# Expert blocks of a hybrid decoder: moving the weight halves between GpSimd, ScalarE and VectorE, and turning the inner rows inside the next gate product

## The reference, cut to what matters

```python
row_tok = jnp.zeros((rows,), jnp.int32).at[dest].set(flat_t[order])
xb = xf[row_tok].reshape(n_blocks, MOE_BLOCK, -1)          # 128 rows x 1024

def expert_block(args):
    xblk, e = args
    return (jax.nn.silu(xblk @ w_gate[e]) * (xblk @ w_up[e])) @ w_down[e]
```

## Time and profile before

| what | value |
|---|---|
| median of three runs | 3995.15 us (3989.59 to 3999.66) |
| time of the profiled execution | 3984.88 us |
| its span, from first to last instruction | 3983.0 us |
| PE busy over the span | 3255.6 us (82%) |
| DVE busy | 1890.7 us (47%) |
| ACT busy | 1362.0 us (34%) |
| POOL busy | 655.6 us (16%) |
| mean granted clock of PE | 0.903 |

### The profile page before, as it was taken

How to read it: one execution, slowest core, us unless ns; L and a number is a source line. 1 busy time by engine, 2 the same in 40 slices (tenths; PEclk the granted TensorE clock), 3 DMA queues, 4 the chain that set the end, 5 groups by cost and what they waited for, 6 DMA issues and landing times. The chain is left out here.

```text
span 3983.0 us, 61834 instructions
## 1 busy us (share of the span) xinstructions
PE 3255.6 (82%) x22582; PEld 2717.2 (68%) x22583; DVE 1890.7 (47%) x2705; ACT 1362.0 (34%) x2830; POOL 655.6 (16%) x425
## 2 busy tenths in 40 slices
PE   7999999899959995486799867885188998989980
PEld 7999999788858884343577725774167777777760
DVE  5252455455535554211466522332377666665634
ACT  5121354355536563032133223442033333333310
POOL 1000000000000001130000010110433534443323
PEclk9999999899979997697899977886599999999995
DMA  4334332334521112353233232222287776776749
GB/s 166 114 108 157 122 109 91 101 118 126 164 85 47 55 50 70 101 184 120 85 120 120 90 109 90 96 93 68 105 290 254 265 282 251 268 271 217 275 167 337
DMA packets 309938, 591.64 MB, mean 149 GB/s; under 512 B 80597, under 2 KB 136323, under 8 KB 309230
## 3 DMA queue, kind: packets, MB, share of 16 engines
q1 hardware_dynamic: 250846, 365.54, 27.7%
q0 software_dynamic: 47776, 196.29, 13.6%
q10 hardware_dynamic: 11136, 27.27, 1.7%
HBM read 462.13 MB, written 160.44 MB: 156 GB/s over the span
## 5 line engine op out<-in xcount | busy, mean ns | idle before, releaser
L136 PE MATMUL pj_pu<-pj_w,pj_nT 128*128 128x256 f32 (+3 forms) x1088 | 306.8, 282 | 0.0
L137 PE MATMUL pj_pu<-pj_w,pj_nT 128*128 128x256 f32 (+3 forms) x1088 | 305.9, 281 | 0.0
L138 PE MATMUL pj_pu<-pj_w,pj_nT 128*128 128x256 f32 (+3 forms) x1088 | 305.3, 281 | 0.0
L2999 POOL TENSOR_TENSOR ex_down<-ex_down_raw,ex_down 128x2048 fp32r<-128x2048 f32 x32 | 212.0, 6625 | 506.9 <-ACT ex_down L3082 506.9
L3103 ACT ACTIVATE ex_y<-ex_py 128x512 f32<-128x512 f32 x96 | 52.2, 597 | 507.6 <-PE ex_py L138 507.6
L137 PEld LDWEIGHTS pj_pu<-pj_w,pj_nT 128*128 128x128 f32 (+1 forms) x1088 | 202.1, 186 | 0.0
L138 PEld LDWEIGHTS pj_pu<-pj_w,pj_nT 128*128 128x128 f32 (+1 forms) x1088 | 202.0, 186 | 0.0
L136 PEld LDWEIGHTS pj_pu<-pj_w,pj_nT 128*128 128x128 f32 (+1 forms) x1088 | 201.7, 185 | 0.1
L136 PE MATMUL ex_py<-ex_down,ex_hT 128*128 128x512 f32 x384 | 156.0, 406 | 40.1 <-POOL ex_down L2999 33.3
L716 ACT ACTIVATE att_prob<-att_score,att_res 128x256 f32<-128x256 f32 (+1 forms) x384 | 127.6, 444 | 144.2 <-DVE att_res L752 144.2
L136 PE MATMUL pj_pu<-pj_nT,pj_w 128*128 128x384 f32 (+2 forms) x480 | 175.3, 365 | 0.0
(11 more groups left out here) (581 smaller groups left out, 8436.6 us busy)
## 6 DMA issues: line engine op xcount, KB each, us to landing
ex_gate_raw<-in_w_gate SPq DMA_DIRECT2D x32, 2048.0 KB
ex_up_raw<-in_w_up SPq DMA_DIRECT2D x32, 2048.0 KB, 11.2
ex_down_raw<-in_w_down POOLq DMA_DIRECT2D x32, 2048.0 KB, 9.3
tmp_yb<-ex_y ACTq DMA_DIRECT2D x48, 512.0 KB, 7.2
out_win_k<-in_cache_k POOLq DMA_DIRECT2D x8, 2032.0 KB, 12.9
out_win_v<-in_cache_v POOLq DMA_DIRECT2D x8, 2032.0 KB, 14.7
tmp_att<-att_res POOLq DMA_DIRECT2D x48, 264.0 KB, 4.6
pout_att<-tmp_att SPq DMA_DIRECT2D x16, 792.0 KB, 7.3
```

What stands on the lines that cost most here:

```text
L136: pe.matmul(out, ah, bh, start=start, stop=False)
L137: pe.matmul(out, ah, bl, start=False, stop=False)
L138: return pe.matmul(out, al, bh, start=False, stop=stop)
L2999: return eng.tensor_tensor(half["d"][:, 1, k], raw["d"][:, k], half["d"][:, 0, k].bitcast(F32), ALU.subtract)
```

## The change

GpSimd computes nothing any more in the loop: it issues gathers, index loads and the loads of d. ScalarE makes the upper half of g as well (`upper_gate`, for block b+2, once the gate product of block b+1 has been done), so it makes all upper halves. VectorE makes all lower halves, for d over all four k-slices. Every half is made in two instructions over half of the k-slices each (`part`), and PE waits for the two separately in the middle of the up and gate products. VectorE's order becomes `hh`, lower d, `hT`, lower u, `rows`, lower g of block b+2. On PE the turn of `hh` moves from ahead of the next gate product to its middle, behind 12 of its 24 matmuls, and PE waits for `sg_ok` before the gate product begins.

```diff
-        def lower_d(eng, n):
-
-            k = slice(n * KF // 2, (n + 1) * KF // 2)
-            return eng.tensor_tensor(half["d"][:, 1, k], raw["d"][:, k], half["d"][:, 0, k].bitcast(F32), ALU.subtract)
+        def part(p, h):
+
+            n = (KF if p == "d" else KD) // 2
+            return slice(h * n, h * n + n)
...
                         for piece, name in (("g", "w_gate"), ("u", "w_up")):
-                            sp.wait_ge(E[piece + "_split"], r)
+                            sp.wait_ge(E[piece + "_split"], 2 * r)
...
                 def work(i, u, b):
                     pool.wait_ge(E["x_turned"], b + 1)
                     gather(u, b + 2, i + 2)
-                    with pool.If(read(pool, 2, b, 1)):
-                        r = began(pool, b)
-                        pool.wait_ge(E["d_hi"], r)
-                        lower_d(pool, 0).then_inc(E["d_split"], 1)
                     with pool.If(read(pool, 2, b + 1, 1)):
                         e = read(pool, 0, b + 1, NE - 1)
-                        r = began(pool, b + 1)
-                        pool.wait_ge(E["d_split"], r)
-                        pool.sem_inc(E["seen"], 1)
-                        pool.wait_ge(E["d_split2"], r)
+                        pool.wait_ge(E["d_split"], 2 * began(pool, b + 1))
                         pool.sem_inc(E["seen"], 1)
                         load_down(e)
...
                 def upper(p, r):
                     act.wait_ge(E[p + "_in"], 16 * r)
-                    act.activation(half[p][:, 0], raw[p][:], ACT.Copy).then_inc(E[p + "_hi"], 1)
+                    for h in range(2):
+                        act.activation(half[p][:, 0, part(p, h)], raw[p][:, part(p, h)], ACT.Copy).then_inc(E[p + "_hi"], 1)
+
+                def upper_gate(b):
+                    with act.If(read(act, 2, b, 1)):
+                        r = began(act, b)
+                        act.wait_ge(E["gate_mm"], b)
+                        act.sem_inc(E["seen"], 1)
+                        upper("g", r)
+
+                upper("g", 1)
                 upper("u", 1)
+                upper_gate(1)
...
                         upper("u", r)
+                    upper_gate(b + 2)
                     act.wait_ge(E["y_mm"], b + 2)
...
-                def halves(p, r):
-                    dve.wait_ge(E[p + "_in"], 16 * r)
-                    split(dve, half[p][:, 0], half[p][:, 1], raw[p][:], E[p + "_hi"], r).then_inc(E[p + "_split"], 1)
-
                 def lower(p, r):
-                    dve.wait_ge(E[p + "_hi"], r)
-                    dve.tensor_tensor(half[p][:, 1], raw[p][:], half[p][:, 0].bitcast(F32), ALU.subtract).then_inc(E[p + "_split"], 1)
+                    for h in range(2):
+                        dve.wait_ge(E[p + "_hi"], 2 * r + h)
+                        dve.tensor_tensor(half[p][:, 1, part(p, h)], raw[p][:, part(p, h)], half[p][:, 0, part(p, h)].bitcast(F32),
+                                          ALU.subtract).then_inc(E[p + "_split"], 1)
+
+                def lower_if(p, b):
+                    with dve.If(read(dve, 2, b, 1)):
+                        lower(p, began(dve, b))
...
                 def work(i, u, b):
-                    with dve.If(read(dve, 2, b + 1, 1)):
-                        dve.wait_ge(E["gate_mm"], b + 1)
-                        halves("g", began(dve, b + 1))
                     dve.wait_ge(E["sg_ok"], b + 1)
                     dve.wait_ge(E["up_mm"], b + 1)
                     dve.wait_ge(E["h_turned"], b + 1)
                     dve.tensor_tensor(hh[:], sg[:], gu[:, 1, :], ALU.mult).then_inc(E["hh_ok"], 1)
-                    with dve.If(read(dve, 2, b, 1)):
-                        dve.wait_ge(E["d_hi"], began(dve, b))
-                        lower_d(dve, 1).then_inc(E["d_split2"], 1)
-                    rows(u, b + 2)
+                    lower_if("d", b)
                     dve.wait_ge(E["h_turned"], b + 2)
                     dve.wait_ge(E["y_mm"], b + 1)
                     split(dve, flat(hT[:, 0]), flat(hT[:, 1]), th[:], E["h_hi"], b + 1).then_inc(E["h_ok"], 1)
-                    with dve.If(read(dve, 2, b + 1, 1)):
-                        lower("u", began(dve, b + 1))
+                    lower_if("u", b + 1)
+                    rows(u, b + 2)
+                    lower_if("g", b + 2)
...
-                def project(p, u, n, b, sem):
-                    pe.wait_ge(E[p + "_split"], began(pe, b) + 1)
-                    for k in range(KD):
-                        last = matmul3(pe, gu[:, n, :], xT[:, u, 0, k, :], xT[:, u, 1, k, :], half[p][:, 0, k, :], half[p][:, 1, k, :],
-                                       k == 0, k == KD - 1)
+                def project(p, u, n, b, sem, between=None):
+                    r = began(pe, b)
+                    for h in range(2):
+                        pe.wait_ge(E[p + "_split"], 2 * r + 1 + h)
+                        if h and between:
+                            between()
+                        for k in range(KD)[part(p, h)]:
+                            last = matmul3(pe, gu[:, n, :], xT[:, u, 0, k, :], xT[:, u, 1, k, :], half[p][:, 0, k, :], half[p][:, 1, k, :],
+                                           k == 0, k == KD - 1)
                     last.then_inc(sem, 1)
...
+                    def turn_h():
+                        pe.wait_ge(E["hh_ok"], b + 2)
+                        for k in range(KF):
+                            last = pe.transpose(th[:, k * P:(k + 1) * P], hh[:, k * P:(k + 1) * P], ident[:])
+                        last.then_inc(E["h_turned"], 1)
+
                     project("u", u, 1, b, E["up_mm"])
                     turn(u, b + 2, i + 2)
-                    pe.wait_ge(E["hh_ok"], b + 2)
-                    for k in range(KF):
-                        last = pe.transpose(th[:, k * P:(k + 1) * P], hh[:, k * P:(k + 1) * P], ident[:])
-                    last.then_inc(E["h_turned"], 1)
-                    project("g", 1 - u, 0, b + 1, E["gate_mm"])
+                    pe.wait_ge(E["sg_ok"], b + 1)
+                    project("g", 1 - u, 0, b + 1, E["gate_mm"], turn_h)
                     r = began(pe, b)
                     pe.wait_ge(E["h_ok"], b + 1)
-                    pe.wait_ge(E["d_split"], r + 1)
-                    pe.wait_ge(E["d_split2"], r + 1)
+                    pe.wait_ge(E["d_split"], 2 * r + 2)
```

More of the change, by code:

```diff
@@ L2968, in experts @@
         py = s.ps("py", [P, 2, 512])
-        names = ("consts_in seen idx_in0 idx_in1 x_in0 x_in1 g_in u_in d_in g_hi u_hi d_hi g_split u_split d_split d_split2 x_turned x_hi x_ok "
+        names = ("consts_in seen idx_in0 idx_in1 x_in0 x_in1 g_in u_in d_in g_hi u_hi d_hi g_split u_split d_split x_turned x_hi x_ok "
                  "gate_mm up_mm sg_ok hh_ok h_turned h_hi h_ok y_mm y_ok y_out0 y_out1 zero_ok zero_out").split()
@@ L3113, in _ @@
             def _(dve):
-                for n in ("g_split", "u_split", "d_split", "d_split2", "hh_ok", "h_turned", "y_mm"):
+                for n in ("g_split", "u_split", "d_split"):
+                    dve.sem_inc(E[n], 2)
+                for n in ("g_hi", "u_hi", "d_hi", "hh_ok", "h_turned", "y_mm"):
                     dve.sem_inc(E[n], 1)
@@ L3131, in rows @@
                     split(dve, flat(xT[:, u, 0]), flat(xT[:, u, 1]), tr[:].rearrange("p k n -> p (k n)"), E["x_hi"], b + 1).then_inc(E["x_ok"], 1)
-                halves("g", 1)
+                lower("g", 1)
                 rows(0, 0)
@@ L3136, in _ @@
                 lower("u", 1)
+                lower_if("g", 1)
                 def work(i, u, b):
-                    with dve.If(read(dve, 2, b + 1, 1)):
-                        dve.wait_ge(E["gate_mm"], b + 1)
-                        halves("g", began(dve, b + 1))
                     dve.wait_ge(E["sg_ok"], b + 1)
```

## The result

The changed kernel took 3896.39 us (median of four, 3885.73 to 3906.32) against 3997.4 for the kernel before, measured beside it (3989.59 to 4006.11): a ratio of 0.9741, 95% interval 0.9713 to 0.9768. The forecast was 3916.

The account below looks back on a forecast made before the run. PE was taken to bound the expert stage. Gains of 9.3 (continuing blocks), 0.6 (last block), 20.5 (new blocks alone) and 48.8 (runs) made 79.2 us off, giving 3905.7 profiled and 3916 as median; range 3889 to 3962, forecast's own 3900 to 3932.

Parts of the forecast that it names:

- Continuing blocks: Fifteen blocks that continue an expert: PE's wait for hh goes, 17.70 us each, 265.5 in all, a gain of 9.3.
- New blocks alone: Nine new blocks standing alone: lower d on VectorE shortens the down product's wait; 18.71 us each, a gain of 20.5.
- rival 3: VectorE's plan reads hide after all, so every new block in a run takes 18.71 us: 3891 in all, chance 0.08.
- VectorE's ring in a run: With new blocks on end, VectorE's instructions and gaps take 20.05 us a block and replace PE as the bound.
- the forecast's 455.5: Time of all 23 new blocks in runs, against 504.3 us before, a gain of 48.8.
- The gathers: Gather issued at 15.6 us into a block, written by 20.5, landed at 24.2, on time for PE by 1.3.
- Rival 1, transfers: DMA transfers pace the runs: 3965 us if runs stay at 504.3, 3940 halfway, 3924 at 358 GB/s; chance 0.20.
- The last rival: ScalarE's strict order: late g weights hold up y copies, Silu and upper d in runs; up to 4018 us, chance 0.05.
- One sign of being wrong: On ScalarE, copies of y standing behind a wait for g's raw weights would show the forecast wrong; no size given.

Follow-up runs that it names:

- e8: The changed kernel with one more VectorE instruction of about 1.2 us, its result unused, behind every lower g: 3913.54 us profiled.
- e6: The changed kernel with ScalarE instead of VectorE making the upper half of the gathered, turned rows: 3893.85 us profiled.
- e4: The changed kernel with every upper and lower piece made in one instruction instead of two halves: 3933.83 us profiled.
- run 361: Not a follow-up run: one whole run of five new blocks in the changed kernel, whose transfers moved 361 GB/s with a DMA share of 0.97.
- e9: The changed kernel with the edits of e5 and e6 together and each gather issued one block earlier on GpSimd: 3887.42 us, ratio 0.9724.
- e12: e9 with every load of d but the first bringing only two of the four k-slices: 3872.35 us, ratio 0.97.
- e11: The changed kernel with each gather issued one block earlier on GpSimd and nothing else changed: 3904.35 us, ratio 0.9769.
- e1: The kernel before with only the turn of the inner rows moved into the middle of the next gate product: 3985.67 us profiled.
- e2: The changed kernel with the turn of the inner rows put back ahead of the gate product: 3901.54 us profiled.
- e3: The changed kernel with the lower half of d's first two slices given back to GpSimd: 3929.18 us profiled.
- e5: The changed kernel with hT made between d's two lower halves and the down product taking d's first two slices first: 3991.03 us profiled.

## Why the prediction came out as it did

*The sign and the parts were right.* Continuing blocks: 274.8 to 265.6 (forecast 265.5). New blocks alone: 169.7 (forecast 168.4); in block 25 the down product began at T 13.28, forecast 13.27, from terms of which two cancel (a gap of 0.84 for 0.76 ahead of d, d itself 4.50 for 4.58).
```profile
3369.18 0.49 PE L136 MATMUL ex_py<-ex_down,ex_hT 128*128 128x512 f32 x1 [0.85 <-DVE ex_hT L131]
```
The 0.14 by which the block is longer is in the down product: it takes 5.57 us behind a wait (3374.75 - 3369.18) and not 5.44, most of it in its first matmul, which took 0.49 there. The time itself, 3896, lies below the forecast's own range of 3900 to 3932, between it and rival 3.

*The mis-sized term is VectorE's ring in a run:* 20.05 forecast, 18.93 measured. By its steps: `hh` and the gap behind it 0.60 in place of 1.45, since the plan's reads for d left no gap where `hh` came straight behind lower g; the three lower pieces 4.40 to 4.41 in place of 4.58, since back-to-back instructions overlap by 0.08; `hT` and its gap 2.24 for 2.16; rows and theirs 2.87 for 2.70. That is 1.12 us. I had read the gap of 0.76 ahead of u, behind `hT`, and took the same behind `hh`; behind `hT` it stands in a run too, behind `hh` it doesn't. The forecast also turns the ring in 17 blocks, and it turns whole in 11: the last block of each run has no lower g ahead of it, and took 18.87, as long as a block alone, not 20.05. Of the 20.0 us by which the runs undercut the forecast's 455.5, the 11 blocks between first and last (18.97 on average) make 11.9, the six last ones 7.1 and the six first ones 1.0. Rival 3, with its 3891 and a chance of 0.08, named part of this: the reads for d hide, those for u and g don't, and the ring stays above the 18.86 of a block alone. e8 shows that the ring still holds the blocks between, e6 that a second limit lies at the same length.

*The gathers* came on time, as forecast, but for another reason, and by luck: the gather shown was written by T 17.2 (3076.67 - 3059.43), not 20.5. Of the 3.3 us some 2.2 are the seam that e4 shows, and 0.9 that it went out at T 14.7 and not 15.6. It landed 5.4 us later, at 3082.06, and not 3.7; PE turned its rows at 3083.93. Written at T 20.5 it would have landed at 3085.3, behind that turn. The Trainium skill (SBUF — State Buffer, Who interferes with whom) has a VectorE instruction with two inputs in SBUF contend with a GpSimd instruction that reads SBUF; the traces agree, 0.98 us against 2.55 and 4.76.

*Rival 1, transfers:* two blocks inside a run of the changed kernel moved 384 GB/s over 38 us with a share of 1.01 (the whole run 361, with 0.97). That is above the 358 GB/s which the Trainium skill gives as a core's half of what an HBM stack delivers (DMA: Bandwidth & Descriptors, Where 436 GB/s comes from), so the measurement decides against that figure as a limit here, with the kernel on one core. They stand right behind VectorE: e9, with VectorE and PE's chain relieved, ran into them, and e12 shows it. Whether fewer bytes alone would shorten the changed kernel's own runs wasn't tried.

*The last rival* didn't show in the changed kernel, where PE never waited for Silu, but decided single blocks of e9, e11 and e12. Why upper g's load comes late in just these blocks stays open. One sign of being wrong did show in the changed kernel, ScalarE's wait for g's raw weights:
```profile
ACT ex_gate L3076 <- DMA ex_gate_raw<-in_w_gate: 30.9, 15, 3.4
```
It cost PE nothing: none of PE's waits in the stage is for ScalarE.

*What isn't shown* is the worth of each part. e1 and e2 test the turn, e3 lower d, e4 the halves; no run gives upper g back to VectorE or puts `rows` back to its old place in VectorE's order, and the parts needn't add up.

## What to carry to other kernels

Read a gap between two instructions in the state that it will be in. In the changed kernel the plan's reads ahead of d cost 0.83 to 0.85 us where VectorE had waited for PE ahead of `hh`, 0.43 to 0.50 in the first block of a run, and nothing in the 11 blocks between its first and its last. Ahead of u, though, a gap of 0.82 to 0.96 stood in every block of a run. It lies behind `hT`, whose second instruction waits for its first; that this is the reason wasn't tried. Count, too, in which blocks a ring turns whole: the last block of a run needs less than the others. Before an edit moves an instruction, follow the loop that its semaphores close through every queue: e5 shortened the block that it aimed at and lost 105 us in runs, because a load on GpSimd waited for what had moved, and a gather stood behind that load. When one engine's order, PE's chain and the transfers all lie within 0.3 us of each other, as here, taking off one of them shows nothing.

## What the runs showed of the hardware that was not expected

A gather that GpSimd issues while VectorE subtracts is held to 0.86 us behind the end of the running instruction, whether that takes 2.29 us or 4.43, and slips in between two subtractions that follow each other without a gap; where a copy from SBUF to SBUF followed, it was held to 0.12 us behind the copy's end. GpSimd's index loads, which are direct transfers, weren't held: in e12 they took 0.55 to 0.57 us under a running subtraction. GpSimd's and VectorE's subtractions exclude each other in whole: a second one, begun 1.8 us behind GpSimd's 4.61, took 5.01 in place of 2.29 (4.61 - 1.8 + 2.29 is 5.10). Pairs of VectorE instructions without a wait between them take 4.49 us where one takes 2.29, an overlap of 0.08 to 0.09. The DMA engines moved 384 GB/s over 38 us, and 361 over the 95 us of a run.
